# RWKV chunk loop: a chunk's other matmuls dealt out between squarings and powers, transposed powers copied by two engines, value part and solve on four array tiles

## Chip, core and metric

One NeuronCore of a Trainium2 chip runs the whole program. The time is device microseconds of one launch; three launches of the kernel before and one profiled execution are given below.

## What is computed

Two layers over 512 tokens of 1024 channels in fp32: RWKV-7 time mixing, then dilated-window attention, each followed by a mixture of 16 SwiGLU experts. The change touches the recurrence of the first layer alone, 16 heads of 64:

```python
def step(state, inp):
    r_t, dec_t, k_t, v_t, kk_t, b_t = inp
    sa = jnp.einsum("bhvk,bhk->bhv", state, kk_t)
    state = (state * dec_t[:, :, None, :]
             - sa[..., None] * b_t[:, :, None, :]
             + v_t[..., None] * k_t[:, :, None, :])
    y_t = jnp.einsum("bhvk,bhk->bhv", state, r_t)
    return state, y_t
_, y = lax.scan(step, state0, (tm(r), tm(decay), tm(k), tm(v), tm(kk), tm(b)))
# then per head: layer norm of y, bonus, gate; x @ w_o and the residual
```

## The kernel before

The program goes in stages: projections, then `rwkv_chunks` (the stage of the change), experts, attention, experts. `rwkv_chunks` cuts the 512 tokens into 8 chunks of 64 (`NC = 8`) and replaces the scan inside a chunk by matrices. All 16 heads (8 pairs `m`, two heads `b` each) go through every step together, mostly as 16 matmuls of 64x64 on tiles of the 128x128 array; the trace shows each fp32 matmul as two records, so x32 there is 16 in the code.

Of chunk c, these groups of matmuls follow from one another:

- `scores` (four rounds of 4 matmuls, L1160) gives keyed products. VectorE masks them into E (`masked`, L1021), ScalarE copies a third part unmasked (`faded`). `plain` (L1170) gives the strictly lower matrix, masked by `lower` (L1027).
- The inverse of a unit triangular matrix is built in levels, function `power`: level lv squares the matrix (L1238) and multiplies the running inverse, from level 1 on together with the transposed matrix (L1249, 64x128). ScalarE copies the squares (`square`) and the transposes (`turned`) back to memory, VectorE adds the inverse's term in three instructions (`inverse`, L1041 and L1044). Levels 0 to 4 square; level 5 gives the inverse `qf`.
- `value_part` (L1184) and `state_part` (L1196, needs the state after chunk c-1) form the right side; ScalarE copies it to `zb`; `solve` (L1203) multiplies it by `qf`; ScalarE copies the solution into VU (`solution`, four instructions).
- `carried` (L1215, the old state) and `advance` (L1221, the chunk's own part) add up output and new state in banks 6 and 7. ScalarE copies the output to Z (`output`), VectorE the state to `sv` (`state`, L1049).

The order is written by hand, one list for each engine, and the engines meet at semaphores (`wait`, with a count per chunk). TensorE works on chunk c's levels and puts chunk c-1's right side, solve, carried and advance between them, and chunk c+1's scores and plain behind level 3. GpSimd makes the start of the inverse (`inverse_start`, L851) and then the keys of two chunks ahead (`keys`, into AR, three deep, and BK, one buffer: L834 to L844). From chunk 3 on VectorE and ScalarE also normalize finished tiles of 128 tokens (`mean`, `center`, `square_of`, `variance`, `root`, `scale`, `gain`, `extra`), which GpSimd's `gates` feed; at the end `turn` and `product` (L1258, L1276) apply w_o.

An operand's place fixes the array tile: the partitions of the inputs give the row half, the partitions of the output the column half.

```python
ins = mm(bank[4 + b][half(l), cols(q, 64)], E[c % 2][half(1 - l), m, b, 0, :], VU[c % 2][half(1 - l), m, b, :], ...)   # value_part
ins = mm(bank[4 + q // GP][half(l), cols(q, 64, 256)], qf[c % 2][half(l), q, :], zb[half(l), q, :], ...)               # solve
```

Of the kernel before, what the change touches and what calls it, by code (L numbers as in the profile page):

```python
# [11 lines left out]
P = 128  # L12
# [8 lines left out]
C = 64  # L21
# [656 lines left out]
def rwkv_chunks(nc, io, g, rw):  # L678
# [9 lines left out]
    with Scope(nc, "chunks") as s:  # L688
# [17 lines left out]
               "zv_done": 1, "zs_done": 1, "u_done": 1, "rec_done": 1,  # L706
               "mk_ok": 8, "la_ok": 8, "n_ok": 2, "q_ok": 15, "s_ok": 2,
               "sq_ok": 10, "nt_ok": 8, "z_ok": 2, "u_ok": 4, "y_ok": 2,
# [15 lines left out]
        score_bank = lambda rd, b: bank[4 + 2 * (rd % 2) + b]  # L724
# [26 lines left out]
        def _(sp):  # L751
# [44 lines left out]
            for c in range(NC + 2):  # L796
                if c < NC:
                    if c >= 2:
                        wait(sp, "rec_done", c - 2, 1)
                    for gr in range(2):  # L800
                        inc(sp.dma_start(VU[c % 2][half(gr), pairs(gr), :, :], tokens(c, gr)), f"v_in{c % 2}")
# [15 lines left out]
            wait(sp, "rec_done", NC - 2, 1)  # L817
# [7 lines left out]
        def _(pool):  # L825
# [4 lines left out]
            def keys(c):  # L830
                at = slice(c * C, c * C + C)
                if c >= 3:
                    wait(pool, "rec_done", c - 3, 1)
# [53 lines left out]
        def _(act):  # L887
# [12 lines left out]
            def turned(c, lv, gr):  # L900
                if gr == 0:
                    wait(act, "pow_done", c, lv + 1)
                elif lv > 0:
                    wait(act, "q_ok", c, 3 * (lv - 1) + 2)
                strip(of_level(lv)[:, pairs(gr), 1, :], bank[gr][:, :].rearrange("p (m x t) -> p m x t", m=GP, x=2)[:, :, 0, :], "nt_ok")

            def faded(c, rd):
                if c >= 2 and rd == 0:
                    wait(act, "rec_done", c - 2, 1)
# [17 lines left out]
            def output(c):  # L927
                wait(act, "rec_done", c, 1)
                if c in (0, 2):
# [5 lines left out]
            def level(c, lv):  # L935
                if lv == 0:
                    square(c, lv)
                    turned(c, lv, 0)
                    turned(c, lv, 1)
                elif lv < 4:  # L940
                    square(c, lv)
                    turned(c, lv, 0)
                    turned(c, lv, 1)
                else:
                    square(c, lv)
# [17 lines left out]
            for c in range(NC + 1):  # L963
                if c < NC:
                    level(c, 0)
                if c in (4, 6, 8):
                    root((c - 4) // 2)
                if c >= 1:
                    right_side(c - 1)
                if c < NC:  # L970
                    level(c, 1)
                if c >= 1:
                    solution(c - 1)
                if c < NC:
                    level(c, 2)
                if c >= 1:
                    output(c - 1)
                if c < NC:
                    level(c, 3)
                    if c < NC - 1:  # L980
                        faded(c + 1, 0)
                        faded(c + 1, 1)
                    if c in (3, 5, 7):
                        square_of((c - 3) // 2)
                    if c == NC - 1:
                        turned_z(0)
                    level(c, 4)
# [3 lines left out]
                    else:  # L991
                        turned_z(1)
            turned_z(2)
# [10 lines left out]
        def _(dve):  # L1004
# [9 lines left out]
            def masked(c, rd):  # L1014
                if c >= 2 and rd == 0:
                    wait(dve, "rec_done", c - 2, 1)
# [11 lines left out]

            def inverse(c, lv):
# [6 lines left out]
                new = (lambda rows, gr: qf[c % 2][rows, pairs(gr), :]) if lv == 5 else (lambda rows, gr: pw[lv % 2][rows, pairs(gr), 2, :])  # L1036
# [3 lines left out]
                for x in range(2):  # L1040
                    inc(nc.vector.tensor_tensor(new(half(x), 1), src(1)[half(x), :, :], old[half(1 - x), pairs(1), 2, :], ALU.add), "q_ok")  # L1041
# [1629 lines left out]
```

## Time and profile before

| | us |
|---|---|
| median of 3 runs (lowest, highest) | 1517.32 (1515.58, 1520.65) |
| profiled execution, its own time | 1514.41 |
| its span | 1512.6 |
| busy in the span: TensorE matmul, VectorE, ScalarE, GpSimd | 1381.7, 1029.8, 856.0, 383.1 |
| this stage on TensorE: first scores to last product | 245.49 to 497.51 |

In the timeline, a row is a run of like instructions: start, length, engine, line, operation, then in brackets how long the engine had been idle before and which instruction ended that. Ends of matmuls are modelled, so a group's cost is best read from its start to the next group's start. In the table of stretches each engine has its busy time and instruction count; PEclk is the granted TensorE clock as a share of 2.4 GHz.

### The profile page before, as it was taken

The page shows a single profiled execution, that of the slowest core. Times are in us where ns is not written, and L with a number is a line of the kernel's source. Part 1 is how long each engine was busy: PE and PEld are TensorE (multiplying, and loading weights), DVE is VectorE, ACT ScalarE, POOL GpSimd, SP SyncE. Part 2 cuts the span into 40 slices and gives each one's busy share as a digit, 9 for nine tenths or more (in the row PEclk, how much of TensorE's full clock was granted, in tenths as well). Part 3 has the DMA queues.
Part 4 walks back from the last instruction along what each step waited for, and adds up shares of the span by engine and source line. Part 5 has one row for each costly group of instructions (what it writes and reads, how often), then busy time and mean ns, then how long its engine had stood idle before and what let it go on. Part 6 is the DMA issues. An engine that isn't in the chain of part 4 may idle for free. (4 is left out here: it accounts for less than half of the span.)

```text
span 1512.6 us, 27566 instructions
## 1 busy us (share of the span) xinstructions
PE 1381.7 (91%) x10579; PEld 1081.2 (71%) x10579; DVE 1029.8 (68%) x1358; ACT 856.0 (57%) x1282; POOL 383.1 (25%) x431
## 2 busy tenths in 40 slices
PE   5999897888899799999999699999989899999994
PEld 2476686777764577888786587778777677888782
DVE  5366644465643599998897535765455799999886
ACT  6635452444431367888885425445453487888882
POOL 1022153546540112222233200001120122222222
PEclk9999897999999899999999899999978899999997
DMA  5222300141550689999996341211102799999985
GB/s 176 84 90 78 139 1 15 50 147 38 172 194 0 226 315 382 382 378 377 383 384 217 115 128 56 81 60 57 56 29 74 286 375 379 380 382 379 379 307 173
DMA packets 160577, 299.64 MB, mean 198 GB/s; under 512 B 16974, under 2 KB 32462, under 8 KB 160481
## 3 DMA queue, kind: packets, MB, share of 16 engines
q1 hardware_dynamic: 147968, 269.43, 49.8%
q0 software_dynamic: 11232, 24.61, 4.6%
q10 hardware_dynamic: 1280, 4.26, 0.7%
q8 instruction: 68, 1.11, 0.3%
q14 instruction: 29, 0.23, 0.0%
HBM read 279.96 MB, written 34.60 MB: 208 GB/s over the span
## 5 line engine op out<-in xcount | busy, mean ns | idle before, releaser
L1443 DVE TENSOR_TENSOR moe_wlo<-moe_raw,moe_whi 128x2048 fp32r<-128x2048 f32 x162 | 370.0, 2287 | 37.4 <-ACT moe_whi L1439 33.0
L1439 ACT ACTIVATE moe_whi<-moe_raw 128x2048 fp32r<-128x2048 f32 x192 | 366.8, 1916 | 23.7 <-PE all_bank L1452 22.4
L1450 PE MATMUL all_bank<-moe_whi,moe_xhi 128*128 128x512 f32 x512 | 208.7, 408 | 4.1 <-DVE moe_xlo L1499 4.1
L1451 PE MATMUL all_bank<-moe_wlo,moe_xhi 128*128 128x512 f32 x512 | 200.8, 392 | 0.0
L1452 PE MATMUL all_bank<-moe_whi,moe_xlo 128*128 128x512 f32 x512 | 200.7, 392 | 0.0
L1450 PEld LDWEIGHTS all_bank<-moe_whi,moe_xhi 128*128 128x128 f32 x512 | 96.8, 189 | 27.6 <-DVE moe_xlo L1499 4.4
L1620 POOL COPY moe_idxcol<-moe_idx 128x1 int32 (+1 forms) x30 | 34.1, 1135 | 315.1 <-PE all_bank L1462 315.1
L1452 PEld LDWEIGHTS all_bank<-moe_whi,moe_xlo 128*128 128x128 f32 x512 | 96.8, 189 | 21.4
L1451 PEld LDWEIGHTS all_bank<-moe_wlo,moe_xhi 128*128 128x128 f32 x512 | 97.1, 190 | 18.2
L1450 PE MATMUL all_bank<-moe_whi,moe_hhi 128*128 128x512 f32 x256 | 100.0, 391 | 3.3 <-issue 2.6
L1451 PE MATMUL all_bank<-moe_wlo,moe_hhi 128*128 128x512 f32 x256 | 99.6, 389 | 0.0
L1452 PE MATMUL all_bank<-moe_whi,moe_hlo 128*128 128x512 f32 x256 | 99.6, 389 | 0.0
L2127 DVE SCALAR_TENSOR_TENSOR attn_wlo<-attn_xhat,all_par,attn_whi 128x512 fp32r<-128x512 f32 x64 | 43.8, 746 | 80.1 <-ACT attn_whi L2110 80.1
L2449 PE MATMUL all_bank<-attn_xhi,attn_whi 128*128 128x512 f32 x192 | 77.8, 405 | 1.5 <-DVE attn_wlo L2121 0.9
L890 ACT ACTIVATE chunks_pw<-all_bank 128x256 f32<-128x256 f32 x144 | 48.4, 384 | 50.5 <-PE all_bank L1238 28.0
L2451 PE MATMUL all_bank<-attn_xhi,attn_wlo 128*128 128x512 f32 x192 | 76.0, 396 | 0.0
L2450 PE MATMUL all_bank<-attn_xlo,attn_whi 128*128 128x512 f32 x192 | 75.8, 395 | 0.0
L1857 DVE TENSOR_TENSOR moe_wlo<-moe_raw,moe_whi 128x1024 fp32r<-128x1024 f32 x60 | 72.9, 1215 | 0.0
L1041 DVE TENSOR_TENSOR chunks_pw<-all_bank,chunks_pw 64x256 f32<-64x256 f32 x64 | 27.0, 422 | 60.0 <-PE all_bank L1249 58.1
L1534 POOL COPY moe_outcol<-moe_outidx 128x1 int32 (+1 forms) x30 | 53.4, 1781 | 23.9 <-DMA out_dram<-moe_yo,moe_outcol 23.8
L358 PE MATMUL all_bank<-project_xhi,project_whi 128*128 128x512 f32 x128 | 52.1, 407 | 7.7 <-DVE rwkv_rw_n L662 4.1
L239 DVE TENSOR_TENSOR project_wlo<-all_h,project_whi 128x2048 fp32r<-128x2048 f32 x12 | 30.3, 2528 | 41.6 <-ACT project_whi L235 41.6
(440 smaller groups left out, 2984.7 us busy)
## 6 DMA issues: line engine op xcount, KB each, us to landing
moe_raw<-in_moe_w_gate_dram SPq DMA_DIRECT2D x64, 1024.0 KB, 9.5
moe_raw<-in_moe_w_up_dram SPq DMA_DIRECT2D x64, 1024.0 KB
moe_raw<-in_moe_w_down_dram SPq DMA_DIRECT2D x64, 1024.0 KB, 8.5
attn_xhat<-in_w_kv_dram SPq DMA_DIRECT2D x10, 1024.0 KB, 5.0
out_dram<-all_gain SPq DMA_DIRECT2D x16, 512.0 KB
attn_xhat<-in_attn_w_q_dram SPq DMA_DIRECT2D x6, 1024.0 KB, 5.0
all_h<-in_rwkv_w_k_dram SPq DMA_DIRECT2D x4, 1024.0 KB, 9.2
all_h<-in_rwkv_w_v_dram SPq DMA_DIRECT2D x4, 1024.0 KB, 5.0
```

Source lines behind the costliest of these rows:

```text
L358: mm(b[:, :], hi[0], hi[1], start=first, stop=False)
L890: inc(nc.scalar.activation(dst, src, ACT.Copy), name)
L1439: nc.scalar.activation(whi[slot % SPLITS][:, :], raw[slot % 6][:, :], ACT.Copy).then_inc(m["hi_ok"], 1)
L1443: nc.vector.tensor_tensor(wlo[slot % SPLITS][:, :], raw[slot % 6][:, :], whi[slot % SPLITS][:, :].bitcast(fp32), ALU.subtract).then_inc(m[ ...
L1450: nc.tensor.matmul(bank[b][:, :], hi[:, k0 + k, :], wh[:, k, :], start=begin and k == 0, stop=False)
L1451: nc.tensor.matmul(bank[b][:, :], hi[:, k0 + k, :], wl[:, k, :], start=False, stop=False)
L1452: ins = nc.tensor.matmul(bank[b][:, :], lo[:, k0 + k, :], wh[:, k, :], start=False, stop=end and k == 3)
L1534: nc.gpsimd.tensor_copy(outcol[:, :], outidx[:, bass.ds(col, 1)]).then_inc(m["oc_ok"], 1)
L1857: ins = nc.vector.tensor_tensor(wlo[slot % SPLITS][:, cols], raw[slot % 6][:, cols], whi[slot % SPLITS][:, cols].bitcast(fp32), ALU.subtract)
L2449: nc.tensor.matmul(out, a[0], b[0], start=begin, stop=False)
L2450: nc.tensor.matmul(out, a[0], b[1], start=False, stop=False)
L2451: return nc.tensor.matmul(out, a[1], b[0], start=False, stop=end)
```

## The change

TensorE's `power` is split into `square` and `power`; `carried`, `advance` and the scores of the next chunk are cut into halves and single rounds, and the twelve pieces of other work stand singly between squarings and powers. The transposed powers of bank 1 are copied by VectorE (`turned`), those of bank 0 by ScalarE. `value_part` and `solve` write and read other halves, so that the four combinations of row half and column half all occur (`rows_of_z`). `carried` and `advance` now fill bank 6 with pairs 0 to 3 and bank 7 with pairs 4 to 7; both output and state are copied by ScalarE, per bank; VectorE's `state` is gone. Score rounds 0 and 1 share banks 4 and 5, rounds 2 and 3 banks 6 and 7 (before they alternated). The normalization steps stand at other places of the lists.

```diff
-        score_bank = lambda rd, b: bank[4 + 2 * (rd % 2) + b]
+        rows_of_z = lambda q, l: l ^ (q // GP)
+        score_bank = lambda rd, b: bank[4 + 2 * (rd // 2) + b]
...
# ScalarE
-            def output(c):
-                wait(act, "rec_done", c, 1)
...
+            def output(c, gr):
+                wait(act, "rec_done", c, 1 + gr)
...
+                strip(Z[c // 2][half(c % 2), pairs(gr), :], bank[6 + gr][0:C, :].rearrange("p (m v) -> p m v", m=GP), "y_ok")
                 for b in range(2):
-                    strip(Z[c // 2][half(c % 2), :, half(b)], bank[6 + b][0:C, :].rearrange("p (m v) -> p m v", m=KT), "y_ok")
+                    strip(sv[half(b), pairs(gr), :], bank[6 + gr][C:P, :].rearrange("p (m b v) -> p m b v", m=GP, b=2)[:, :, b, :], "s_ok")
...
# VectorE
+            def turned(c, lv):
+                wait(dve, "pow_done", c, lv + 1)
+                inc(nc.vector.tensor_copy(of_level(lv)[:, pairs(1), 1, :], bank[1][:, :].rearrange("p (m x t) -> p m x t", m=GP, x=2)[:, :, 0, :]), "nt_d")
...
# TensorE, scores(c, rd)
-                if rd < 2:
-                    if c >= 2:
-                        wait(pe, "y_ok", c - 2, 2)
-                        wait(pe, "s_ok", c - 2, 2)
-                else:
-                    wait(pe, "mk_ok", c, 2 * rd - 2)
-                    wait(pe, "la_ok", c, 2 * rd - 2)
+                if rd % 2:
+                    wait(pe, "mk_ok", c, 2 * rd)
+                    wait(pe, "la_ok", c, 2 * rd)
+                elif c >= 2 and rd == 0:
+                    wait(pe, "u_ok", c - 2, 4)
+                elif c >= 2:
+                    wait(pe, "y_ok", c - 2, 2)
+                    wait(pe, "s_ok", c - 2, 4)
...
# value_part, solve
-                    ins = mm(bank[4 + b][half(l), cols(q, 64)], E[c % 2][half(1 - l), m, b, 0, :], VU[c % 2][half(1 - l), m, b, :], start=q % GP == 0, stop=False)
+                    ins = mm(bank[4 + b][half(rows_of_z(q, l)), cols(q, 64)], E[c % 2][half(1 - l), m, b, 0, :], VU[c % 2][half(1 - l), m, b, :], start=q % GP == 0, stop=False)
...
-                    ins = mm(bank[4 + q // GP][half(l), cols(q, 64, 256)], qf[c % 2][half(l), q, :], zb[half(l), q, :], start=True, stop=True)
+                    at = half(rows_of_z(q, l))
+                    ins = mm(bank[4 + q // GP][half(l), cols(q, 64, 256)], qf[c % 2][at, q, :], zb[at, q, :], start=True, stop=True)
```

TensorE's list, one regular chunk (here chunk 2's levels with chunk 1's other work). L1238 are squarings, L1249 powers, L1196 state part, L1203 solve, L1215 carried, L1221 advance, L1160 scores. Before:

```order
L1238 MATMUL all_bank<-chunks_low,all_h 64x64 x16
L1249 MATMUL all_bank<-all_h,chunks_low 64x64 x16
L1196 MATMUL all_bank<-chunks_sv,rwkv_rw_tmp 64x64 x16
L1238 MATMUL all_bank<-chunks_pw 64x64 x16
L1249 MATMUL all_bank<-chunks_pw 64x128 x16
L1203 MATMUL all_bank<-chunks_zb,chunks_qf 64x64 x16
L1215 MATMUL all_bank<-chunks_sv,rwkv_rw_tmp 128x64 x16
L1238 MATMUL all_bank<-chunks_pw 64x64 x16
L1249 MATMUL all_bank<-chunks_pw 64x128 x16
L1221 MATMUL all_bank<-chunks_vu,chunks_keyed 128x64 x16
```

Now the squarings are L1248, the powers L1263, the others L1192, L1200, L1217, L1226 and L1156:

```order
L1248 MATMUL all_bank<-chunks_low,all_h 64x64 x16
L1192 MATMUL all_bank<-chunks_sv,rwkv_rw_tmp 64x64 x16
L1263 MATMUL all_bank<-all_h,chunks_low 64x64 x16
L1217 MATMUL all_bank<-chunks_sv,rwkv_rw_tmp 128x64 x8
L1248 MATMUL all_bank<-chunks_pw 64x64 x16
L1200 MATMUL all_bank<-chunks_zb,chunks_qf 64x64 x16
L1263 MATMUL all_bank<-chunks_pw 64x128 x16
L1217 MATMUL all_bank<-chunks_sv,rwkv_rw_tmp 128x64 x8
L1248 MATMUL all_bank<-chunks_pw 64x64 x16
L1226 MATMUL all_bank<-chunks_vu,chunks_keyed 128x64 x8
L1263 MATMUL all_bank<-chunks_pw 64x128 x16
L1156 MATMUL all_bank<-rwkv_rw_tmp 128x192 x4
```

Solve stands before the power of level 1 and not behind it, and advance is in two halves, the first of them behind level 2's squaring and the second behind level 3's.

ScalarE's list from the output of chunk 1 on: `chunks_pw` are squares (from banks 2 and 3) and transposes (banks 0 and 1), `chunks_keyed` the `faded` copies. Before:

```order
L890 ACTIVATE rwkv_rw_w<-all_bank6 64x8x64
L890 ACTIVATE rwkv_rw_w<-all_bank7 64x8x64
L890 ACTIVATE chunks_pw1<-all_bank2 128x4x64
L890 ACTIVATE chunks_pw1<-all_bank3 128x4x64
L890 ACTIVATE chunks_pw1<-all_bank0 128x4x64
L890 ACTIVATE chunks_pw1<-all_bank1 128x4x64
L890 ACTIVATE chunks_keyed<-all_bank5 128x2x64
L890 ACTIVATE chunks_keyed<-all_bank4 128x2x64
L890 ACTIVATE chunks_keyed<-all_bank7 128x2x64
L890 ACTIVATE chunks_keyed<-all_bank6 128x2x64
L890 ACTIVATE chunks_pw0<-all_bank2 128x4x64
L890 ACTIVATE chunks_pw0<-all_bank3 128x4x64
```

Now, from the copies of level 3's squares on:

```order
L891 ACTIVATE chunks_pw1<-all_bank2 128x4x64
L891 ACTIVATE chunks_pw1<-all_bank3 128x4x64
L891 ACTIVATE rwkv_rw_w<-all_bank7 64x4x128
L891 ACTIVATE chunks_sv<-all_bank7 64x256 x2
L891 ACTIVATE chunks_pw1<-all_bank0 128x4x64
L891 ACTIVATE chunks_keyed<-all_bank5 128x2x64
L891 ACTIVATE chunks_keyed<-all_bank4 128x2x64
L891 ACTIVATE chunks_pw0<-all_bank2 128x4x64
L891 ACTIVATE chunks_pw0<-all_bank3 128x4x64
```

The output comes in two portions with the state's copies beside it, and one round's `faded` copies stand directly ahead of the copies of level 4's squares.

## Rows read from the trace of the kernel before

**Rows 1.** Busy time by stretch: us, then each engine, PEclk, DMA share, GB/s.

```profile
245.50:252.20 6.70, 5.87 (x64) 5.15 (x64) 3.68 (x10) 2.22 (x8) 0.58 (x1) 0.65 0.01 2
252.30:269.70 17.40, 12.44 (x448) 10.71 (x448) 9.65 (x25) 8.03 (x26) 8.86 (x12) 1.00 0.01 3
269.80:290.80 21.00, 19.44 (x576) 17.65 (x576) 11.01 (x27) 10.86 (x34) 10.56 (x17) 1.00 0.24 69
337.80:364.20 26.40, 21.40 (x576) 19.11 (x576) 15.01 (x32) 12.64 (x36) 14.57 (x14) 0.94 0.14 53
411.20:454.30 43.10, 39.75 (x688) 29.91 (x689) 20.05 (x29) 14.37 (x38) 21.94 (x12) 1.00 0.57 199
```

**Rows 2.** Waits in the stage: who waited for whom, total us, times, longest.

```profile
PE all_bank L1160 <- DVE chunks_sv L1049: 4.0, 3, 3.2
PE all_bank L1249 <- POOL chunks_pw L851: 0.9, 2, 0.6
```

**Rows 3.** Timeline of TensorE over one regular chunk: start, length, row.

```profile
269.76 0.69 PE L1238 MATMUL all_bank<-chunks_low,chunks_keyed 64*64 64x64 f32 x32 [0.36 <-DVE chunks_low L1027]
...
274.39 2.00 PE L1215 MATMUL all_bank<-chunks_sv,rwkv_rw_tmp 64*128 64x64 f32 x32
276.32 0.69 PE L1238 MATMUL all_bank<-chunks_pw 64*64 64x64 f32 x32
276.84 1.06 PE L1249 MATMUL all_bank<-chunks_pw 64*64 64x128 f32 x32
277.82 3.79 PE L1221 MATMUL all_bank<-all_h 128*128 128x64 f32 x32
281.54 0.69 PE L1238 MATMUL all_bank<-chunks_pw 64*64 64x64 f32 x32
...
283.21 1.57 PE L1160 MATMUL all_bank<-chunks_ar,rwkv_rw_tmp 64*128 64x192 f32 x16
284.71 0.69 PE L1238 MATMUL all_bank<-chunks_pw 64*64 64x64 f32 x32
...
288.05 0.92 PE L1160 MATMUL all_bank<-chunks_ar,rwkv_rw_tmp 64*128 64x192 f32 x8
288.90 0.69 PE L1170 MATMUL all_bank<-rwkv_rw_tmp,chunks_ar 64*64 64x64 f32 x32
289.43 1.10 PE L1184 MATMUL all_bank<-chunks_vu,chunks_keyed 64*64 64x64 f32 x32
290.88 0.33 PE L1238 MATMUL all_bank<-chunks_low,all_h 64*64 64x64 f32 x6 [0.36 <-DVE chunks_low L1027]
```

**Rows 4.** Timeline of ScalarE: solution copies, and two copies of squares.

```profile
274.97 1.57 ACT L890 ACTIVATE all_h<-all_bank 64x256 f32<-64x256 f32 x4
285.71 0.66 ACT L890 ACTIVATE chunks_pw<-all_bank 128x256 f32<-128x256 f32 x2
```

**Rows 5.** Timeline of VectorE: the first two adds of a level's inverse, and the third.

```profile
277.96 0.88 DVE L1041 TENSOR_TENSOR chunks_pw<-all_bank,chunks_pw 64x256 f32<-64x256 f32 x2 [2.85 <-PE all_bank L1249]
278.87 0.43 DVE L1044 TENSOR_TENSOR chunks_pw<-all_bank,chunks_pw 128x256 f32<-128x256 f32 x1
```

**Rows 6.** Timeline of GpSimd: from a chunk's inverse start to the next keys.

```profile
269.12 3.12 POOL L851 TENSOR_TENSOR chunks_pw<-chunks_keyed,all_ident 64x256 f32<-64x256 f32 x4 [8.24 <-DVE chunks_keyed L1021]
...
277.07 1.34 POOL L843 TENSOR_TENSOR rwkv_rw_tmp<-rwkv_rw_k,rwkv_rw_xT 128x256 f32<-128x256 f32 x2
```

**Rows 7.** Timeline of chunk 4: TensorE's longest wait, a table load, VectorE's gain.

```profile
339.90 1.28 ACT L955 ACT_TABLE_LOAD   x1
352.35 1.22 DVE L1072 TENSOR_TENSOR rwkv_rw_w<-rwkv_rw_w,rwkv_rw_k 128x1024 f32<-128x1024 f32 x1 [4.17 <-POOL rwkv_rw_k L868]
355.17 2.13 PE L1160 MATMUL all_bank<-chunks_ar,rwkv_rw_tmp 64*128 64x192 f32 x16 [3.17 <-DVE chunks_sv L1049]
```

**Rows 8.** Timeline of the stage's start: the four rounds of scores, first masks.

```profile
245.49 5.25 PE L1160 MATMUL all_bank<-rwkv_rw_tmp 64*128 64x192 f32 x32 [5.85 <-POOL rwkv_rw_tmp L836]
...
247.19 0.76 DVE L1021 TENSOR_TENSOR all_h<-all_bank,all_chmask 128x256 f32<-128x256 f32 x2 [2.67 <-PE all_bank L1160]
```

More of the change, by code:

```diff
@@ L970, in _ @@
                 if c < NC:
[L971 removed]
+                    square(c, 1)
+                    turned(c, 1)
                 if c >= 1:
@@ L1229, in power @@
                     wait(pe, "sq_ok", c, 2 * lv)
-                    wait(pe, "nt_ok", c, min(2 * lv, 8))
-                rows = lambda q, l: half(at_level(q, l, lv))
-                out = lambda q, l: half(at_level(q, l, lv + 1))
-                now = of_level(lv - 1)
-                plain_at = lambda q, l: low[rows(q, l), q, :] if lv == 0 else now[rows(q, l), q, 0, :]
-                turned_at = lambda q, l: E[c % 2][rows(q, l), pair_at(q, l), q // GP, 0, :] if lv == 0 else now[rows(q, l), q, 1, :]
-                if lv < 5:
-                    for q, l in places:
-                        ins = mm(bank[2 + q // GP][out(q, l), cols(q, 64)], turned_at(q, l), plain_at(q, l), start=True, stop=True)
-                    inc(ins, "sq_done")
+                    wait(pe, "nt_a", c, lv)
+                    wait(pe, "nt_d", c, lv)
+                plain_at, turned_at, _, out = level_of(c, lv)
+                for q, l in places:
+                    ins = mm(bank[2 + q // GP][out(q, l), cols(q, 64)], turned_at(q, l), plain_at(q, l), start=True, stop=True)
+                inc(ins, "sq_done")
+            def power(c, lv):
                 if lv == 0 and c >= 1:
@@ L1245, in power @@
                     wait(pe, "q_ok", c, 3 * (lv - 1))
+                if lv == 5:
+                    wait(pe, "sq_ok", c, 10)
+                plain_at, _, both_at, out = level_of(c, lv)
                 lo, hi = (1, 2) if lv == 0 else (1, 3) if lv < 4 else (2, 3)
                 for q, l in places:
-                    moving = turned_at(q, l) if lv == 0 else now[rows(q, l), q, lo:hi, :].rearrange("p x t -> p (x t)")
-                    ins = mm(bank[q // GP][out(q, l), cols(q, 128)][:, 64 * (lo - 1):64 * (hi - 1)], plain_at(q, l), moving, start=True, stop=True)
+                    ins = mm(bank[q // GP][out(q, l), cols(q, 128)][:, 64 * (lo - 1):64 * (hi - 1)], plain_at(q, l), both_at(q, l), start=True, stop=True)
                 inc(ins, "pow_done")
@@ L1288, in _ @@
                 if c < NC:
-                    power(c, 1)
+                    power(c, 0)
+                if c >= 1:
+                    carried(c - 1, 0)
+                if c < NC:
+                    square(c, 1)
                 else:
@@ L1293, in _ @@
                     solve(c - 1)
-                    carried(c - 1)
                 if c < NC:
-                    power(c, 2)
+                    power(c, 1)
+                if c >= 1:
+                    carried(c - 1, 1)
+                if c < NC:
+                    square(c, 2)
                 else:
@@ L1299, in _ @@
                 if c >= 1:
-                    advance(c - 1)
+                    advance(c - 1, 0)
+                if c < NC:
+                    power(c, 2)
+                    if c < NC - 1:
+                        scores(c + 1, 0)
+                    square(c, 3)
+                if c >= 1:
+                    advance(c - 1, 1)
                 if c < NC:
```

185 lines of the change are left out of this document (97 added, 88 removed).

## The prediction

> **What bounds the kernel now.** I read first the busy time by stretch, and of it only the chunk stage, since nothing else is edited. It takes 252 us of TensorE's time. In a regular chunk TensorE is busy 19.44 of 21.00 us, VectorE 11.01, ScalarE 10.86, GpSimd 10.56; from the last chunk's levels on it is busy 39.75 of 43.10 [rows 1]. So TensorE bounds the stage, with short waits on the copies of its own results. Then the waits: two kinds in the stage are no part of the regular pattern, 4.0 us for the state's copy by VectorE (3.2 of them at once) and 0.9 us for GpSimd's inverse start [rows 2].
>
> Then the timeline of a chunk without disturbance. From one chunk's first squaring to the next is 290.88 - 269.76 = 21.12 us. From start to start, a group of 16 matmuls 64x64 takes 0.52 (276.32 to 276.84), a power with 128 columns 0.98, carried 1.93, advance 3.72, two rounds of scores together 1.50, one round by itself 0.85, the value part 1.03 (a row of 1.10, less the 0.07 by which a row exceeds the distance to the next) [rows 3]. I take 1.03 for solve too, which has the same form on two tiles. Summed: 5 squarings 2.60; powers 3 x 0.52 + 3 x 0.98 = 4.50; state part 0.52; solve 1.03; carried 1.93; advance 3.72; scores 1.50 + 0.85 + 0.85 = 3.20; plain 0.53; value part 1.03. That is 19.06, so 2.06 us of a chunk are waits.
>
> **The change in a regular chunk.** Value part and solve have the operands' halves so mixed that all four tiles occur, as in the squarings, which take 0.52 for 16: I take 0.52 each, a gain of 1.02. Scores in four single rounds cost 4 x 0.85 = 3.40, 0.20 more [rows 3]: 1.50 against 1.70 says that each visit to a wider form costs 0.2 once. Carried and advance are also cut, two visits more; bounds 0 and 0.2 each, I take 0.1, as parts of a visit already lie in the rows they leave. Work: 19.06 - 1.02 + 0.20 + 0.20 = 18.44.
>
> Now the waits that the new order leaves. Two are worked out in full.
> - First half of advance behind solve. Solve 0.52, power 1 0.98, second half of carried 0.97, squaring 0.52: TensorE stands ready 2.99 after solve's start. ScalarE first copies the transposes of power 1 (ready 0.52 + 1.06 + 0.07 after solve's start), 0.28 to the next instruction, then four copies of the solution, 1.57 [rows 4], and 0.15 to TensorE (my estimate for a hand-over to it; the one from TensorE to ScalarE I take at the 0.07 by which rows overlap the distance): 3.65. A wait of 0.66; before, carried and a level covered it.
> - Plain of the next chunk needs the copies of level 4's squares. They stand on ScalarE behind a `faded` copy that waits for VectorE's mask, and that behind the inverse's three adds, 0.88 + 0.43 [rows 5], and VectorE's new copy, 0.33. From power 3's start: 1.06 + 0.07 + 0.33 + 1.31 + 0.41 (mask) + 0.3 (faded copy) + 0.66 (two copies of squares, [rows 4]) + 0.2 for two hand-overs = 4.34. TensorE has power 3 0.98, scores 0.85, squaring 0.52, scores 0.85 and power 4 0.52 = 3.72 (3.8 with a form change) to do. A wait of 0.55.
> - The same kind of chain leaves 0.4 at the first squaring of a chunk (0.36 now), 0.2 at power 0, 0.1 at the last scores and 0.3 at power 5. Bounds for these four together: 0.4 and 1.5; I take 1.05.
>
> Sum 2.3. Period 18.44 + 2.3 = 20.7 to 20.9, against 21.12: 0.25 less. **Over six regular chunks -1.5.** The removed `state` of VectorE (0.7 for each bank) was covered, apart from chunk 4; the state's copies on ScalarE are covered too, since score rounds 2 and 3 alone need them. VectorE gains four copies and loses two of double length, ScalarE the reverse; neither gets above 12 of 21 us.
>
> GpSimd: from a chunk's last mask to the next keys is 269.12 to 278.41, 9.3 us [rows 6]. In the new order the first score round stands at about 0.52 + 0.52 + 0.52 + 0.97 + 0.52 + 0.52 + 0.98 + 0.97 + 0.52 + 1.86 + 0.98 = 8.9 plus waits of 0.9 behind the first squaring, where it was 12.3 behind; GpSimd begins 0.6 ahead of that squaring. Cover is left in every regular chunk, about 1 us. It is gone in chunk 0, whose levels have nothing between: the round waits about 1.6 there. But chunk 0 also loses waits for ScalarE, which copies half as many transposes; I count it at 17.2 for 17.5, **-0.3**.
>
> **Normalization.** In chunk 4 TensorE waited 3.17 for the state, because VectorE stood at a gain that waited 4.17 for GpSimd, and afterwards ran at half clock: scores 2.13 instead of 1.57 [rows 7], a granted clock of 0.94 over the chunk [rows 1], about 1.3 us. With the rest of the 4.0 and the 0.9 of GpSimd, 6.2 us are to be had. The new list puts other things in their place. `root` with its table load, 1.28 + 0.3, stands directly ahead of a transposed copy: ScalarE needs 0.07 + 1.3 (three output copies) + 1.6 + 0.4 + 0.15 = 3.5 behind the first half of advance, TensorE has 0.98 + 0.85 to do: 1.6 of wait, in chunks 4 and 6. Gain and extra, 2 x 1.25 [rows 7], stand ahead of VectorE's copy of level 0: 2.5 + 0.42 + 0.15 against 0.15 + 0.52 + 1.05 on TensorE, 1.4 of wait, in chunks 5 and 7. Together 6.0. **Net -0.2**; the bounds are -4 (they fall into waits that are there anyway) and +2.
>
> **The start.** Rounds 0 and 1 of scores now share banks, so round 1 waits for round 0's mask, and round 3 for round 2's. Four rounds took 5.25, 1.3 each; the masks of round 0 end at 247.19 + 0.76 = 247.95 [rows 8]. Round 1 starts at 248.1 instead of 246.8, round 3 loses as much or, at full clock, 0.9: **+2.2** (1.7 to 2.6). **The end.** From the last chunk's levels TensorE is nearly always busy; value part and solve bring their 1.0: **-1.0**.
>
> Sum: -1.5 - 0.3 - 0.2 + 2.2 - 1.0 = -0.8. The profiled execution (1514.4, 1.8 above its span) would be 1513.6. The median of the runs, 1517.3, is 2.9 higher; from it I forecast **1516.5**. About 0.3%, 4.6 us, is what a measurement of this kernel can tell from no change; -0.8 lies inside.
>
> **Rivals.**
> - *The pieces cover the copies after all.* Waits go down from 2.06 a chunk to about 1.6 and the extra visits are free: a period of 20.0 instead of 20.8, -4.8 more over six chunks, and half of the normalization's 6.0 falls into those waits. 1509. For it: twelve points instead of six at which a copy can run beside other work, VectorE and ScalarE half idle [rows 1]. Against it: the list of squarings, masks and copies stays a serial chain whose links I added up.
> - *The clock.* The stage starts at a granted share of 0.65 [rows 1]. The new start has two pauses of 1 us more between its rounds, and chunk 0 is busy only 12.44 of 17.40. If the clock stays at 1.2 GHz through chunk 0, its groups take up to 1.7 times as long where they bound it; at 5 to 6 us of path that way, 1522. It decides if the rise comes after the first squaring, 254 us, instead of about 250. Against it: chunk 0 had pauses of 1.5 us before and the share is 1.00.
> - *Changes of tile form cost more.* By my rows a visit is 0.2, and three are added. At 0.2 for all, 0.2 a chunk more and the time 1517.9. To get past 0.3% slower it takes 0.5 a visit. The Trainium skill (TensorEngine Tiling (Array Packing), "Key Properties") says that changing the tiling mode, not just the tile, drains TensorE, which speaks against cutting the wide groups; by that rule every one of the three visits pays in full and my sum is 1517.9 instead of 1516.5. The trace agrees for scores and cannot show it for the others.
> - *The four tiles do not run at once.* Then 16 times 0.52 are not gained: 1524.8. Against it: squarings write the same mix of halves into one bank in 0.52.
>
> **How the numbers follow.** Forecast 0.50 (1513 to 1520); cover 0.27; clock 0.10; tile form at more than 0.2 a visit 0.08, of which 0.03 still inside 0.3%; four tiles not at once 0.05. Faster 0.27, same 0.53, slower 0.20. The range of 1508.5 to 1521.5 holds the forecast, nearly all of cover and part of the clock.
>
> **What would show it.** Right: value part and solve at 0.52; period of a regular chunk 20.5 to 21.0; TensorE waiting some 0.6 for `chunks_vu` or `all_h` ahead of each first advance; waits of 1.4 to 1.6 in chunks 4 to 7 for a table load's and for gain's successor; first squaring at 254.5, not 252.3. Wrong: a period under 20.2 (the chains overlap where I added them), or over 21.4 with no wait that names an engine (form changes), or a PEclk under 1.00 in chunk 0.

## The result, and the profile after

The changed kernel took 1531.69 us (median of 8 runs, 1525.83 to 1540.18), the kernel before 1517.8 beside it (8 runs): a ratio of 1.0094, 95% interval 1.0066 to 1.0122. It is slower by about 14 us, where -0.8 was forecast, and lies 10 us above the end of the range. The profiled execution took 1528.97 us with a span of 1527.2, 14.6 more than before. All of it arises in the chunk stage: from the first score block to the last product of the projection it is 251.6 us before and 266.5 after.

The stage of both kernels, busy time by stretch (us, busy time of PE, PEld, DVE, ACT, POOL, then the granted clock PEclk, DMA share, GB/s). Before, the whole stage and the part from the first squaring on:

```profile
245.40:497.00 251.60, 222.42 (x4768) 175.63 (x4768) 128.91 (x255) 99.72 (x291) 108.58 (x103) 0.98 0.28 91
252.20:497.00 244.80, 216.54 (x4704) 170.47 (x4704) 125.23 (x245) 97.50 (x283) 107.96 (x102) 0.99 0.29 93
```

After, the same two, then three stretches of it (chunk 1, regular; chunk 3; a piece of chunk 3 at the low level), to be held against [rows 1]:

```profile
245.60:512.10 266.50, 235.87 (x4768) 180.88 (x4768) 131.69 (x271) 102.71 (x291) 108.55 (x102) 0.93 0.27 86
255.90:512.10 256.20, 228.58 (x4704) 175.17 (x4704) 127.91 (x261) 100.49 (x283) 107.58 (x101) 0.94 0.28 89
...
273.70:295.00 21.30, 20.13 (x576) 17.35 (x576) 11.41 (x30) 11.26 (x34) 10.65 (x16) 1.00 0.21 55
...
319.90:348.20 28.30, 25.92 (x591) 22.53 (x583) 14.10 (x29) 11.48 (x35) 11.55 (x11) 0.76 0.28 88
...
325.00:340.00 15.00, 15.00 (x223) 13.43 (x212) 7.82 (x12) 6.04 (x17) 6.60 (x6) 0.54 0.02 4
```

The number of TensorE's instructions is the same (x4768), yet TensorE is busy 13.5 us longer, and PEclk is 0.93 instead of 0.98. TensorE is granted 2.4 or 1.2 GHz (1.00 or 0.50 in this column), so a PEclk of p over a length L means 2 x (1 - p) x L at 1.2 GHz: 10 us of the stage before, 37 after (to within 3, by the column's rounding). That is the first half of the finding.

The second half is in the waits. Who waited for whom in the stage before (us in total, times, longest; the two waits of [rows 2] left out, and smaller ones):

```profile
PE all_bank L1238 <- ACT chunks_pw L890: 6.8, 10, 1.5
...
PE all_bank L1249 <- DVE chunks_pw L1044: 4.6, 7, 0.7
...
PE all_bank L1238 <- DVE chunks_low L1027: 3.0, 7, 0.9
PE all_bank L1238 <- issue: 2.6, 2, 1.7
PE all_bank L1184 <- issue: 1.3, 1, 1.3
```

and after (smaller ones left out):

```profile
PE all_bank L1263 <- issue: 4.6, 4, 1.8
PE all_bank L1217 <- issue: 3.4, 3, 1.7
PE all_bank L1263 <- DVE chunks_pw L1044: 3.2, 11, 0.6
PE all_bank L1248 <- ACT chunks_pw L891: 3.0, 3, 1.7
PE all_bank L1192 <- issue: 2.5, 2, 1.4
PE all_bank L1248 <- issue: 2.1, 1, 2.1
PE all_bank L1156 <- DVE all_h L1016: 2.1, 2, 1.1
PE all_bank L1180 <- issue: 1.9, 1, 1.9
```

Waits that name an engine went from 20.5 us to 13.4. Of this 4.9 are the two waits of [rows 2], which are gone, and 2.1 came in at the start; what is left, 4.3, is mostly copies that the pieces now cover. But rows with "issue", time in which TensorE waited for nothing that the profile shows, went from 8.2 us (8 times) to 15.2 (12 times). What was won on the one side was lost on the other, and the clock came on top.

How such a pause looks. TensorE of the changed kernel (start, length, row, idle before it with its releaser): first one in chunk 1's state part, then the two after which the clock fell, and a squaring behind that fall (1.13 for 0.69).

```profile
295.56 0.63 PE L1192 MATMUL all_bank<-chunks_sv,rwkv_rw_tmp 64*64 64x64 f32 x26
297.30 0.28 PE L1192 MATMUL all_bank<-chunks_sv,rwkv_rw_tmp 64*64 64x64 f32 x3 [1.11 <-issue]
...
319.69 0.40 PE L1180 MATMUL all_bank<-all_h 64*64 64x64 f32 x12 [1.93 <-issue]
...
324.30 0.21 PE L1217 MATMUL all_bank<-chunks_sv,chunks_ar 64*128 64x64 f32 x1 [1.72 <-issue]
...
329.00 1.13 PE L1248 MATMUL all_bank<-chunks_pw 64*64 64x64 f32 x32
```

They cut a group in the middle, the first one after 26 of its 32 multiplications and loads, where no semaphore stands. From one pause to the next, busy time by stretch:

```profile
297.28:301.17 3.89, 3.25 (x127) 2.87 (x126) 0.42 (x1) 1.59 (x5) 3.74 (x5) 1.00 0.02 6
319.67:324.28 4.61, 2.89 (x126) 2.69 (x127) 0.42 (x1) 1.59 (x5) 4.42 (x5) 1.00 0.49 147
350.48:354.29 3.81, 3.14 (x127) 2.87 (x126) 1.55 (x2) 1.59 (x5) 3.66 (x5) 1.00 0.01 4
373.05:377.28 4.23, 2.43 (x126) 2.25 (x126) 3.92 (x6) 0.81 (x3) 3.71 (x4) 1.00 0.01 4
```

Always 126 or 127 multiplications and as many loads, and 3.8 to 4.6 us. The DMA queue of kind "instruction" over 245.6 to 440 reads

```profile
q8 instruction: 35, 0.57, 1.2%
```

thirty-five packets of 16 KB. In the same time TensorE had 4318 multiplications and as many loads, 123 of each to a packet, close to the 126 between pauses. I take it that one packet holds 126 pairs and a few instructions between them, and call the place where one packet's instructions end a seam. The instructions of a packet lasted 3.8 us or more in these stretches, while a group of 32 pairs 64x64 takes 0.52: 126 such pairs are through in 2.05.

The trace's DMA records tie the packets to the pauses. Behind the pause that ends at 297.30 the next packet runs from 298.75 to 299.76, and the next pause ends at 301.18. All twelve pauses of the changed kernel end 1.3 to 1.6 us after such a packet is through. In the kernel before seven of the eight do (1.2 to 1.5); the eighth, 0.67 at L1276, stands at no seam. From the end of a pause at a seam it was at least 1.0 us to the next packet's start in every trace, and a packet took at least 0.88.

Counted in multiplications from the first score block, the twelve pauses stand behind 1146, 1273, 1649, 1775, 2277, 2404, 2781, 2907, 3033, 3409, 4038 and 4542 of them, apart by multiples of 125.8 to within two. A chunk has 576 ([rows 1]), which is no multiple of that, so the seams fall on other groups in each chunk. The expectations below count by 503, which is four packets, and call it a chunk's records: their places 15, 141, 267 and 392 are the ends of four packets in turn, not places of a chunk.

### The profile page after: what moved, and what is told of

Same layout as the page of the kernel before. It is cut to its first block and busy times, and to the rows that moved or that the text cites. A ratio compares the mean times of both kernels' runs of the same rounds, so it can differ in the third digit from the quotient of the medians.

```text
span 1527.2 us, 27612 instructions
## 1 busy us (share of the span) xinstructions
PE 1393.5 (91%) x10579; PEld 1084.4 (71%) x10579; DVE 1032.6 (68%) x1374; ACT 859.0 (56%) x1282; POOL 382.2 (25%) x431
## 5 line engine op out<-in xcount | busy, mean ns | idle before, releaser
L891 ACT ACTIVATE chunks_pw<-all_bank 128x256 f32<-128x256 f32 x112 | 38.6, 382 | 49.3 <-PE all_bank L1248 26.2
L1026 DVE COPY chunks_pw<-all_bank 128x256 f32<-128x256 f32 x32 | 13.6, 424 | 74.3 <-PE all_bank L1263 74.3
## 6 DMA issues: line engine op xcount, KB each, us to landing
moe_raw<-in_moe_w_up_dram SPq DMA_DIRECT2D x64, 1024.0 KB, 10.3
```

## The experiments

**Theory A, the start:** the new waits in the first rounds, at the low level. **Theory B, supply of instructions:** dense 64x64 groups use up a packet faster than the next is there; shorter groups and fewer other waits turn into pauses, and pauses bring the low clock. **Theory C:** changes of tile form. Rival to B: chance, or DMA load of the zero rows.

**a_start.** Chunk 0's score rounds back on alternating banks:

```diff
-score_bank = lambda rd, b: bank[4 + 2 * (rd // 2) + b]
+score_bank = lambda c, rd, b: bank[4 + 2 * (rd % 2 if c == 0 else rd // 2) + b]
```

(and chunk 0's waits as in the kernel before).

> The changed kernel with one thing put back: in chunk 0 alone the rounds of score blocks go over two pairs of score banks in turn, as before. Theory A (the start: two rounds that wait for VectorE's row maxima, 1.06 and 1.04 us, in a phase at the low clock): the first squaring comes about 6.8 us after the stage begins instead of 10.3, and the time falls by 3 to 4 us, to about 1528. Theory B (instruction supply: TensorE's own pauses of 0.3 to 2.1 us inside groups, 15 us in all after against 8 before, and the clock that they cost): these stay at 15 us in sum, and the time stays 10 us above the kernel before. If the pauses are mere chance from one execution to the next, their places and their sum differ here by several us, with nothing changed behind chunk 0.

Measured: 1530.39 us, ratio to the kernel before 1.0097 (1.0068 to 1.0127). In the trace the start is won back, the score blocks run without a wait and the first squaring stands 6.76 us after them, where it stood 10.27 in the changed kernel:

```profile
245.88 5.26 PE L1160 MATMUL all_bank<-rwkv_rw_tmp 64*128 64x192 f32 x32 [5.85 <-POOL rwkv_rw_tmp L837]
...
252.64 0.69 PE L1252 MATMUL all_bank<-chunks_low,all_h 64*64 64x64 f32 x32 [0.89 <-DVE chunks_low L1022]
```

(The "row maxima" of the expectation are the masks, L1016.) The time does not show it, though a gain of 3.5 us is less than the 6 us to which two such ratios tell kernels apart. The pauses sum to 12.5. The trace, which is of the slowest of the 10 executions, spends 23.9 us at 1.2 GHz twice, the first time from within a pause of 2.03 on that ends at 323.17, and its stage from the first squaring on is 268.1 us.

```profile
322.30:346.20 23.90, 23.03 (x321) 20.32 (x320) 10.24 (x18) 8.34 (x23) 9.27 (x9) 0.50 0.14 47
```

A is right on its 3.5 us in the trace and, at that size, can't explain the 14.

**a_two.** The changed kernel with value part and solve on two tiles:

```diff
-        rows_of_z = lambda q, l: l ^ (q // GP)
+        rows_of_z = lambda q, l: l
...
-   ins = mm(bank[4 + b][half(l ^ b), cols(i, 64)], AR[c % 3][half(b), m, 0, :], ...
+   ins = mm(bank[4 + b][half(l), cols(i, 64)], AR[c % 3][half(b), m, 0, :], ...
```

> The changed kernel with the value part and the solve on two tiles as before. Without a limit of the instruction supply this makes each chunk slower by some 1.0 us (the two groups took about 0.5 us less each on four tiles) and the time 8 us longer, about 1540. Theory B, that TensorE outruns its instructions: what these groups lose comes back as shorter pauses and fewer low-clock stretches, so the time is the same or shorter, 1524 to 1533. Theory C, that changing from one tile form to another costs 0.3 to 0.6 us a chunk: part of the 8 us comes back too, but with the pauses' sum as long as in the changed kernel, time 1535 to 1537.

Measured: 1528.95 us, ratio 1.0082 (1.0051 to 1.0114). The 8 us are not there, and the time lies where theory B had it. But the pauses sum to 14.0 (15.2 on four tiles), and by PEclk 44 us of the stage are at 1.2 GHz, so the trace shows no shorter pauses or low stretches that would have given them back. Something else does: the undisturbed chunk takes 21.66 us on two tiles (272.52 to 294.18) and 21.42 on four. The two groups are busy 0.9 longer (1.1 each, for 0.7 and 0.6), and two waits for VectorE, of 0.24 and 0.25, are gone. So in the new order half of what four tiles save is spent on waits for VectorE.

**b_four.** The kernel before with that part alone.

```diff
-  ins = mm(bank[4 + b][half(l), cols(q, 64)], E[c % 2][half(1 - l), m, b, 0, :], ...
+  ins = mm(bank[4 + b][half(l ^ b), cols(q, 64)], E[c % 2][half(1 - l), m, b, 0, :], ...
...
+  at = half(l ^ (q // GP))
+  ins = mm(bank[4 + q // GP][half(l), cols(q, 64, 256)], qf[c % 2][at, q, :], zb[at, q, :], ...
```

> The kernel before with one part of the change alone: value part and solve on four tiles. If TensorE's own time decides, a chunk gets 1.0 us shorter and the kernel 8 us faster, about 1510. Theory B (instruction supply): the groups are shorter, but the pauses inside groups grow from 8 us in sum by about as much, with low-clock stretches behind them: 1515 to 1525. Theory C (tile forms): the group rows themselves show what switching costs, as groups beside them that take longer than in the kernel before.

Measured: 1517.02 us, ratio 1.0012 (0.9982 to 1.0042). No gain. Groups of one undisturbed chunk (268.2 to 289.4 before, 266.1 to 287.4 here; busy us, mean ns, idle before). Before:

```profile
L1184 PE MATMUL all_bank<-all_h 64*64 64x64 f32 x32 | 1.1, 218 | 0.0
L1203 PE MATMUL all_bank<-chunks_zb,chunks_qf 64*64 64x64 f32 x32 | 1.1, 218 | 0.0
...
L1238 PE MATMUL all_bank<-chunks_low,chunks_keyed 64*64 64x64 f32 x32 | 0.7, 224 | 0.4 <-DVE chunks_low L1027 0.4
```

b_four:

```profile
L1204 PE MATMUL all_bank<-chunks_zb,chunks_qf 64*64 64x64 f32 x32 | 0.7, 218 | 0.0
L1239 PE MATMUL all_bank<-chunks_low,chunks_keyed 64*64 64x64 f32 x32 | 0.7, 224 | 0.8 <-DVE chunks_low L1027 0.8
...
L1184 PE MATMUL all_bank<-all_h 64*64 64x64 f32 x32 | 0.6, 218 | 0.0
```

The four tiles run at once, 0.9 us is saved on the two groups, and 0.4 of it is at once a longer wait for VectorE's `low`. The pauses did not grow as B expected: 8.4 us in sum, for 8.2. PEclk of the stage is 0.94, 31 us at 1.2 GHz instead of 10, so in this trace the rest went into the clock.

**a_warm.** Three 128x512 multiplications ahead of the first score block.

```diff
+            for _ in range(3):
+                mm(bank[7][:, :], g["ident"][:, :], w[:, 0, :], start=True, stop=True)
             for rd in range(4):
                 scores(0, rd)
```

> The changed kernel with three 128x512 multiplications into an unused PSUM bank ahead of the first score block, where TensorE is otherwise idle. If the low clock of the first rounds is a matter of what TensorE did before, the clock rises before or within the first rounds; the rounds that wait for VectorE's row maxima keep their waits, but the ten microseconds up to the first squaring, and the first squares, get shorter: 2 to 4 us off, about 1528. If the waits alone decide, nothing changes or it adds the 1 us of the three.

Measured: 1530.16 us, ratio 1.0106 (1.0055 to 1.0157). From the first score block to the first squaring it is 7.26 us instead of 10.27, with both waits of 1.06 still there; the score block begins at 246.88, about a microsecond late, behind the three. The execution with the profile happened to be the fastest, 1514.54, the others were 1528.88 and more. It shows what this order can do when the clock stays up, with pauses of 11.8 in all:

```profile
254.10:498.90 244.80, 220.43 (x4704) 167.74 (x4704) 127.68 (x261) 100.39 (x283) 108.69 (x102) 0.98 0.29 93
```

244.8 us from the first squaring on, just what the kernel before has.

**a_sh32, a_sh64, a_sh96.** The test of the seams: the same work, moved along in TensorE's program.

```diff
+            for _ in range(32):      # 64, 96
+                mm(bank[7][0:64, 0:16], g["ident"][0:64, 0:64], w[0:64, 0, 0:16], start=True, stop=True)
             for rd in range(4):
                 scores(0, rd)
```

> The changed kernel with 32 tiny multiplications (64x64 by 16 columns, into an unused bank) in TensorE's idle time ahead of the first score block; everything behind them is the same, only 64 instructions further on in TensorE's program. Pauses of 0.3 to 3 us stand in the changed kernel after every 126th load and multiplication, always at the same places of a chunk (records 141, 267 and 392 of its 503, and 15). If they are the seams between pieces of TensorE's instructions, they move to 109, 235, 360 and 486 of the chunk, and their lengths and the time change with what work surrounds them there: between 1505 and 1545. If they belong to the work (a group, a wait, a bank), they stay where they were and the time stays at 1530.

> As with 32, but 64 of the tiny multiplications: by the seams, the pauses stand at 77, 203, 328 and 454 of the chunk's 503 records, between the places of the changed kernel; the seam that stood in the run of short groups (value part, squaring, state part, power) now stands 64 records earlier. Time between 1505 and 1545; with pauses that belong to the work, 1530 and the same places.

> As with 64, but 96: by the seams, pauses at 45, 171, 296 and 422. Of the three shifts and the changed kernel (shift 0) one should have clearly fewer or shorter pauses and less time at 1.2 GHz than the others if the place of the seams in the chunk matters; if supply is limited on the average over a chunk, all four have the same 13 to 17 us of pauses.

Each of the tiny multiplications is two in the trace, like all of this kernel's, so the shifts are 64, 128 and 192 pairs, twice what the expectations count, and their places don't apply. By half a packet, a whole one, and one and a half, the seams should stand half-way for 32 and 96 and where they were for 64. They did. With 64 all ten pauses stand behind the same multiplications as in the changed kernel or at whole packets from them (1146, 1273, 1775 and on). With 32 they stand behind 1336, 1712, 2214, 2341 and 3472, each 63 from an old seam, and with 96 at seams half-way too (1336, 1712, 2341, 3472 and others). Besides, two pauses of 0.2 to 0.3 in each of these two traces stand at no seam, in rounds of scores. One stretch of a_sh32, busy time between two pauses:

```profile
345.24:348.57 3.33, 2.50 (x127) 2.29 (x126) 1.64 (x4) 1.62 (x6) 3.08 (x4) 1.00 0.03 8
```

| kernel | shift in pairs | first squaring, us | pauses in the stage | at 1.2 GHz in the stage | time | ratio to before (95%) |
|---|---|---|---|---|---|---|
| changed kernel | 0 | 255.91 | 15.2 | 37 | 1531.69 | 1.0094 (1.0066 to 1.0122) |
| a_sh64 | 128 | 263.16 | 13.4 | 26 | 1536.43 | 1.0163 (1.0121 to 1.0204) |
| a_sh32 | 64 | 256.84 | 7.7 | 48 | 1521.55 | 1.0046 (1.0029 to 1.0063) |
| a_sh96 | 192 | 270.65 | 7.7 | 15 | 1536.47 | 1.0165 (1.0128 to 1.0201) |

The added work delays the start by 7.3, 0.9 and 14.7 us. With that taken off the ratios' distance from 1 (times 1515), 14.2 and 17.4 us stay with the old seams and 6.1 and 10.3 with the new: the place of the seams is worth 8 us, with an uncertainty of about 5 from the four intervals. That the start's delay counts in full is taken for granted here; a_sh32, with nothing taken off, is 7 us (give or take 5) under the changed kernel. The work and its order are the same in all four. Half of the pauses go, with the seams in other groups. The low clock of the single traces doesn't go along with the times.

**a_late.** The changed kernel with the zero rows sent after the chunk loop:

```diff
-                if 2 <= c < 10:
-                    blank_rows(2 * c - 4)
-                    blank_rows(2 * c - 3)
...
+            for e in range(16):
+                blank_rows(e)
             sp.wait_ge(blank_st, 16 * 16)
```

> The changed kernel with the sixteen transfers of zero rows (512 KB each) issued after the chunk loop, ahead of the wait for them, instead of two a chunk from chunk 2 on. If the pauses come from instruction packets that queue behind these transfers, they shrink from 15 us in sum to under 5 in the chunk loop, and the stage from the first score block to the last product gets at least 8 us shorter than the changed kernel's 266. If DMA load has no part in them (a pause of 1.1 us stood at 297 with the engines at 2% of their time), sum and places stay. The whole time may be longer by what the late transfers then hold up.

Measured: 1523.24 us, ratio 1.0044 (1.0018 to 1.0069), 7.6 us better than the changed kernel, with an uncertainty of about 6. Pauses 7.6 us instead of 15.2, at the old seams; under 5 was expected. The stage got shorter by only 3.6 in the trace (PEclk 0.91), where at least 8 was expected. So load on the DMA engines isn't the pauses' cause: they are still there, and three of the four stretches above between pauses had a DMA share of 0.02 or less. Whether it lengthens them is not shown: the packets of instructions took as long (37 of them 1.05 us in the mean in the changed kernel, 1.06 here).

**b_sh32 and b_late.** The same two edits in the kernel before.

> The kernel before with 32 tiny multiplications ahead of the first score block (64 loads and 64 multiplications in TensorE's program, half the distance of two seams; about 1 us later start). The same shift made the changed kernel 10 us faster with the start's delay left out. If the kernel before stands well by the luck of its seams, it gets slower here, to 1520 to 1530, with pauses 64 records from their old places (142, 268 and 396 of the chunk's 503) and longer; if half-way seams are better for any order of this work, it gets faster, 1505 to 1512; if its order leaves the seams less to do wherever they stand, 1514 to 1518.

> The kernel before with the sixteen transfers of zero rows after the chunk loop. In the changed kernel this took 7.6 us off, and the share of it that is a faster supply of instructions or other loads should be had here too, though its pauses are half as long: 1508 to 1513. If the gain came from a clock that stayed up by chance, no difference, 1515.

Measured: b_sh32 1519.07 us, ratio 1.0004 (0.9976 to 1.0031), pauses 10.7, again half a packet from the old ones but for the one at L1276, which stayed with its group; b_late 1513.17, ratio 0.9986 (0.996 to 1.0011), pauses 5.3. The kernel before does not live on the luck of its seams, to within 4 us, and the late transfers may help it by 2 us, which these runs can't tell from nothing.

**a_comb.** The changed kernel with a_start's banks, 32 tiny multiplications and the late zero rows.

> The changed kernel with the three edits together: chunk 0's rounds on alternating banks, 32 tiny multiplications for the seams, zero rows after the chunk loop. Single, they gave 0 to -1, -10 and -7.6 us. If they add, 1512 to 1515, and the stage from the first score block to the last product is at 250 us; if the shift and the late transfers act on the same pauses, only the larger of them counts, 1519 to 1522.

Measured: 1522.41 us, ratio 1.0033 (1.0009 to 1.0057). They do not add; pauses 9.6, more than the 7.7 of a_sh32 in spite of the late transfers, and PEclk 0.91. It does not beat the kernel before, and no version here does so measurably.

**after2.** The changed kernel again, for a second trace.

> The changed kernel once more, unaltered, for a second trace. If the pauses stand at seams of TensorE's instructions, they are again at records 15, 141, 267 and 392 of a chunk's 503 and nowhere else, though their lengths and which of them show may differ by a microsecond or more, and the low-clock stretches with them; if they were chance or came from transfers that happened to be under way, other places show up too. Stage from the first score block to the last product 257 to 274 us, as in the traces of the changed kernel and of its near copies.

Measured: 1530.8 us. Eleven pauses, 16.8 in sum, all at the seams of the first trace and ten of them behind the very same multiplications; their lengths differ from the first trace's (1.9 at 297.24, where it had 1.1; none at 319). 43 us of the stage at 1.2 GHz.

## Why the prediction was wrong

Where the stage got longer, in the two traces (us):

| part | forecast | measured |
|---|---|---|
| start, to the first squaring | +2.2 | +3.5 (6.76 to 10.27) |
| chunk 0 | -0.3 | +0.2 (17.51 to 17.75) |
| six regular chunks with normalization | -1.7 | +8.0 (141.4 to 149.5) |
| from the last chunk's levels on | -1.0 | +3.2 (85.8 to 89.0) |

The change of the stage by kind, put together from the same traces: waits on engines -7.1, pauses +7.0, the low clock +27 us of length, at up to half of it +13.6, and +1.4 that is left; sum +14.9. It is an account with a bound in it (not all work at 1.2 GHz is TensorE's), and some 4 us more of work (see the regular chunk) belong into it, so the clock's part is rather 11. It is still the largest item. The runs say so too: over the 8 executions of the changed kernel the mean granted clock is 0.937 to 0.948, and the 1525.83 one has 0.947, the 1540.18 one 0.937. Their mean is 0.943, while the kernel before has 0.953 to 0.955 in the 61 executions beside the later runs. Inside the changed kernel a line through the 8 gives 1.07 us for each 0.001 (0.9 to 1.5 in the other kernels run five times or more), which makes 11 us of the 0.010 between the two. This is an estimate: longer pauses may come with a lower clock in the same execution.

- **What bounds the kernel.** "TensorE bounds the stage, with short waits on the copies of its own results" left out a kind that was in the same view: 8.2 us of "issue", in eight pauses. I read only the waits that named an engine. This is the step that failed: the sum has no term for these pauses (+7.0 measured) and none for the clock behind the start (at 1.2 GHz 37 us for 10, some 11 of length), though the prediction had read one such fall in chunk 4 and priced it at 1.3. TensorE at 0.52 us for 32 pairs was already past its supply of instructions in bursts, and time saved on a 64x64 group or on a wait ahead of one could turn into a pause.
- **Value part and solve.** The groups behaved: the value part from 294.18 to 295.08 less a wait of 0.25, so 0.65, against 1.09 before by the same reading (0.52 for 1.03 in the forecast), and solve 0.48, all four tiles at once. The two saved 0.9 of the 1.02. A chunk got 0.5 of it in the old order and 0.24 in the new one (b_four, a_two).
- **A regular chunk.** Forecast 20.7 to 20.9, measured 295.08 - 273.66 = 21.42, against 21.12 before. The waits were over-estimated: 0.38 ahead of the first advance for 0.66, 0.24 and 0.25 at power 5 and the first squaring, 1.2 in all, with gaps too short for a row of waits, where I had 2.3. (So counted, the chunk before had 1.6 of waits and not the 2.06 that the prediction got by subtracting.) The work was under-estimated, 20.2 for 18.44. (The prediction's own sum is 20.74, which over six chunks is -2.3; it took -1.5.) The rows, against [rows 3]:

```profile
280.97 2.01 PE L1226 MATMUL all_bank<-all_h 128*128 128x64 f32 x16 [0.38 <-ACT all_h L891]
282.91 1.10 PE L1263 MATMUL all_bank<-chunks_pw 64*64 64x128 f32 x32
283.94 0.92 PE L1156 MATMUL all_bank<-chunks_ar,rwkv_rw_tmp 64*128 64x192 f32 x8
284.92 0.69 PE L1248 MATMUL all_bank<-chunks_pw 64*64 64x64 f32 x32
285.55 2.00 PE L1226 MATMUL all_bank<-all_h 128*128 128x64 f32 x16
...
290.96 0.69 PE L1263 MATMUL all_bank<-chunks_pw 64*64 64x64 f32 x32
291.68 0.69 PE L1166 MATMUL all_bank<-rwkv_rw_tmp,chunks_ar 64*64 64x64 f32 x32
292.51 0.92 PE L1156 MATMUL all_bank<-chunks_ar,rwkv_rw_tmp 64*128 64x192 f32 x8
```

  From start to start a half advance is 1.94 (1.86 forecast), a round of scores 0.98 where a squaring follows (0.85 forecast), a squaring ahead of an advance 0.63, plain ahead of scores 0.83 (0.52). Of these 0.06 is a gap that ScalarE's copies end, in the 0.98, and 0.14 one that nothing named ends, in the 0.83. With gaps taken off, the chunk's work went from 19.5 to 20.2 though value part and solve lost 0.9: the other groups took 1.6 more, the squarings 0.6 of it, scores 0.35, carried and advance 0.3, powers 0.25, plain 0.15. The forecast had 0.4. That is the third rival (0.2 to 0.5 a visit), which I gave 0.08 (its 1517.9, 0.2 a chunk on 1516.5, should read 1517.7): over its three visits 1.6 is 0.5 each. The chunk is 0.3 longer where 0.25 less was forecast: some 3 us over six. The Trainium skill (TensorEngine Tiling (Array Packing), "Key Properties") says that TensorE drains when the tiling mode changes; the trace agrees in sign, with the 1.6 us. That the whole of it is a drain was not tried by itself.
- **Normalization.** The wait behind the table load came as worked out: 1.6 forecast, 1.68 in chunk 4. In chunk 6 it was 0.39, and those behind gain and extra, 1.4 each, did not show; in chunk 7 another of 0.91. So the waits of this term were shorter than forecast, and that gain is in the -7.1.

```profile
361.09 1.28 ACT L942 ACT_TABLE_LOAD   x1
...
363.20 0.69 PE L1248 MATMUL all_bank<-chunks_pw 64*64 64x64 f32 x32 [1.68 <-ACT chunks_pw L891]
```

- **The start.** +2.2 forecast, +3.5 measured (6.76 to 10.27). Two waits as forecast, of 1.06 and 1.04; the rest is the last round of scores and plain at 1.2 GHz (1.65 and 1.13 long, 0.92 and 0.69 at full clock). The rival "The clock" had its condition fulfilled (rise at 260.8 instead of 250.2, behind the first squaring) and 1522 as its time. It was right on this place and did not see the later falls. The wait for GpSimd's keys that chunk 0 was to have didn't come, behind a start that was later by 3.5.

```profile
245.64 1.65 PE L1156 MATMUL all_bank<-rwkv_rw_tmp 64*128 64x192 f32 x8 [5.85 <-POOL rwkv_rw_tmp L837]
248.35 2.93 PE L1156 MATMUL all_bank<-rwkv_rw_tmp 64*128 64x192 f32 x16 [1.06 <-DVE all_h L1016]
252.32 1.65 PE L1156 MATMUL all_bank<-rwkv_rw_tmp 64*128 64x192 f32 x8 [1.04 <-DVE all_h L1016]
253.91 1.13 PE L1166 MATMUL all_bank<-rwkv_rw_tmp 64*64 64x64 f32 x32
255.91 0.38 PE L1248 MATMUL all_bank<-chunks_low,all_h 64*64 64x64 f32 x4 [0.88 <-DVE chunks_low L1022]
```

- **The end.** -1.0 forecast, +3.2 measured: it has pauses of 1.70 and 1.34 where the kernel before had 0.81 and 0.67, and a stretch at 1.2 GHz from 428.0 on where that had none.

**What stays open.** That the pauses are waits for packets of instructions is shown by their places and by the packets' times, and that the place of the seams costs time by the shifts. That they bring the low clock is argued from the order of events: in the first trace the clock falls at 325.6, 400.7 and 428.0, behind pauses of 1.93 and 1.72, 2.13, and 1.70; before, at 390.2 behind one of 1.71. But it also fell at 356.0 before, behind the wait of 3.17 for VectorE, and at 362.0 in a_two behind one of 1.67 for ScalarE, so a pause at a seam isn't needed. And a pause of 1.81 at 377.3, or one of 2.30 at 349.39 in after2, had no such fall, and the sums don't go together across traces (a_warm: 11.8 of pauses, 10 us at the low level; a_sh32: 7.7 and 48). What the low clock costs is clearer. From the first squaring on the stage is 244.8 us in a_warm and 245.3 in a_sh96, with PEclk 0.98 in both, and 244.8 at 0.99 in the kernel before; it is 256.2 and 258.6 in the changed kernel at 0.94, and 268.1 in a_start at 0.89. How long it stays low, 3 or 24 us, differs between executions of one program, and one trace each can't settle what decides it. The combination still lies 5 us above the kernel before; which of form changes, pauses and clock holds them is open as well. An order of the groups in which dense ones never fill a packet wasn't tried.

## What to carry to other kernels

A row of waits that names nobody is a bound like any other: where an engine runs many short instructions, look whether its pauses stand a fixed number of instructions apart and cut groups in the middle. If so, work saved on the short groups may not be saved, and it is a check worth one run to put a few idle instructions ahead and see whether the pauses move. Hold the pauses against the times of the instruction queue's packets too. Cutting long groups into pieces to cover copies had a price of its own here, 1.6 us a chunk in the groups beside the cuts. That it also took away waits in which the supply caught up is my reading and was not tried by itself.

## What was not expected of the hardware

TensorE's instructions came in packets of 16 KB with 126 pairs of load and multiplication each, and in bursts one packet's instructions took 3.8 to 4.6 us from pause to pause, or 3.3 with the seams elsewhere (a_sh32), of which TensorE was busy 2.4 to 4.0. A pause at a seam ended 1.2 to 1.7 us after a packet was through, in all fourteen traces, and was 0.15 to 3.2 us long. Tiny multiplications with no waits between them go 128 pairs to a packet: 128 of them ahead left the pauses where they were. Moving identical work by 64 such pairs changed a kernel of 1530 us by 8, give or take 5. And one program, a_late, ran from 1514.99 us at a mean granted clock of 0.954 to 1528.5 at 0.943 with nothing changed: 13.5 us for 33 us more at 1.2 GHz, which is as large as the whole effect that was studied.
